# One decoder layer on one core: x and the first weights loaded in alternating pieces, the low-rank gate product behind the first chunk

## What is computed

```python
proj = h @ w_in
qa, ka, va, qg, kg, vg, rg, glr = jnp.split(proj, cuts, axis=-1)
log_a = jax.nn.log_sigmoid((glr @ w_gate_up + b_gate).astype(jnp.float32)) / GLA_GATE_TEMP
o = _gla(_heads(qg, GLA_HEADS), _heads(kg, GLA_HEADS), _heads(vg, GLA_HEADS), _heads(log_a, GLA_HEADS))
```

## Time and profile before

| | before |
|---|---|
| median of 3 runs | 429.07 us (428.97 to 429.78) |
| span of the profiled execution | 427.1 us |
| TensorE matmuls busy | 409.8 us, 96% |
| TensorE weight loads busy | 363.5 us, 85% |
| VectorE busy | 276.7 us, 65% |
| ScalarE busy | 195.3 us, 46% |
| POOL busy | 69.0 us, 16% |
| transferred | 75.64 MB, mean 177 GB/s |

### The profile page before, as it was taken

How to read it: one execution, slowest core, us unless ns; L and a number is a source line. 1 busy time by engine, 2 the same in 40 slices (tenths; PEclk the granted TensorE clock), 3 DMA queues, 4 the chain that set the end, 5 groups by cost and what they waited for, 6 DMA issues and landing times.

```text
span 427.1 us, 6338 instructions
## 1 busy us (share of the span) xinstructions
PE 409.8 (96%) x2576; PEld 363.5 (85%) x2576; DVE 276.7 (65%) x322; ACT 195.3 (46%) x243; POOL 69.0 (16%) x62
## 2 busy tenths in 40 slices
PE   7899999998999999799999999999999999999993
PEld 2899977888988888699988689898989898989882
DVE  2638377798596699966766875554555546372727
ACT  4644486843335637326543626344343444444400
POOL 1092000019681104100005220000000000000005
PEclk9899999999999999999999999999999999999997
DMA  8985638555146282274544264647373746555002
GB/s 244 397 326 190 206 101 293 185 198 167 44 142 261 93 282 110 92 264 140 196 152 144 100 196 165 231 146 248 106 265 122 231 162 200 193 172 221 0 2 98
DMA packets 33159, 75.64 MB, mean 177 GB/s; under 512 B 2528, under 2 KB 5104, under 8 KB 33136
## 3 DMA queue, kind: packets, MB, share of 16 engines
q1 hardware_dynamic: 31776, 75.18, 50.8%
q10 hardware_dynamic: 1360, 0.15, 0.3%
HBM read 74.27 MB, written 1.05 MB: 176 GB/s over the span
## 4 chain that ended last, share of the span: by engine, by line
PE 64%; DVE 5%; ACT 3%; issue 2%; POOL 1%; DVEq 0%; ACTq 0%
PE bank L1204 20%; PE bank L1206 20%; PE bank L1205 20%; DVE w_lo L797 1%; ACT w_hi L509 1%; PE bank L1360 1%; ACT again L656 1%; POOL actA_lo L483 1%; DVE X L1010 1%; DVE X L1016 1%; DVE actA_lo L1035 1%; ACT actA_hi L661 1%; DVE stats L998 0%; PE bank L1418 0%; DVE X L993 0%
## 5 line engine op out<-in xcount | busy, mean ns | idle before, releaser
L797 DVE TENSOR_TENSOR w_lo<-raw,w_hi 128x2048 fp32r<-128x2048 f32 x36 | 83.8, 2334 | 31.0 <-ACT w_hi L509 31.0
L1204 PE MATMUL bank<-actA_hi,w_hi 128*128 128x256 f32 x352 | 99.9, 284 | 0.6 <-DVE actA_lo L1035 0.6
L1205 PE MATMUL bank<-actA_lo,w_hi 128*128 128x256 f32 x352 | 99.6, 283 | 0.0
L1206 PE MATMUL bank<-actA_hi,w_lo 128*128 128x256 f32 x352 | 99.6, 283 | 0.0
L1138 DVE TENSOR_TENSOR w_lo<-raw,w_hi 128x2048 fp32r<-128x2048 f32 x24 | 55.0, 2291 | 44.8 <-ACT w_hi L739 44.8
L509 ACT CAST w_hi<-raw 128x2048 fp32r<-128x2048 f32 x38 | 72.1, 1912 | 16.5 <-PE bank L1206 14.2
L1204 PE MATMUL bank<-w_hi,actB_hi 128*128 128x512 f32 x192 | 75.5, 393 | 0.0
L1205 PE MATMUL bank<-w_lo,actB_hi 128*128 128x512 f32 x192 | 74.8, 390 | 0.0
L1206 PE MATMUL bank<-w_hi,actB_lo 128*128 128x512 f32 x192 | 74.7, 389 | 0.0
L1204 PEld LDWEIGHTS bank<-actA_hi,w_hi 128*128 128x128 f32 x352 | 67.5, 192 | 1.6 <-issue 1.3
L1205 PEld LDWEIGHTS bank<-actA_lo,w_hi 128*128 128x128 f32 x352 | 67.5, 192 | 0.3
(11 more groups left out here) (174 smaller groups left out, 599.6 us busy)
## 6 DMA issues: line engine op xcount, KB each, us to landing
raw<-in_w_ff SPq DMA_DIRECT2D x32, 1024.0 KB, 5.2
raw<-in_w_in SPq DMA_DIRECT2D x10, 1024.0 KB, 8.1
raw<-in_w_xkv SPq DMA_DIRECT2D x8, 1024.0 KB, 5.1
raw<-in_w_mix_o SPq DMA_DIRECT2D x4, 1024.0 KB, 4.9
raw<-in_w_xq SPq DMA_DIRECT2D x4, 1024.0 KB, 5.4
raw<-in_w_xo SPq DMA_DIRECT2D x4, 1024.0 KB, 5.0
raw<-in_w_in SPq DMA_DIRECT2D x4, 512.0 KB, 9.3
probs<-in_ln_g SPq DMA_DIRECT2D x3, 512.0 KB, 6.2
```

The costliest lines, as they stand in the source:

```text
L797: dve.tensor_tensor(dst, half_view(u), hi_part.bitcast(f32), ALU.subtract).then_inc(lo_done, 1)
L1204: pe.matmul(dst, stat[0], mov[0], start=start, stop=False)
L1205: pe.matmul(dst, stat[0], mov[1], start=False, stop=False)
L1206: return pe.matmul(dst, stat[1], mov[0], start=False, stop=stop)
```

## The change

It does five things.

- SP loads x in four pieces of 0.25 MB and chunk 0 in four pieces of 0.5 MB, alternating. The list `EARLY_CUTS` says in which pieces ScalarE and VectorE split them, and `early_count` which count of the counters belongs to a piece. TensorE works through chunk 0 k by k, all four column groups of one k together; high x high and high x low of a k are ahead of the wait for that k's low weights.
- The low-rank product goes behind chunk 0. Its weights come from the host as a contiguous array `w_glr`, and are split in high and low: 16 columns each in a stationary tile of 128 columns whose rest POOL has set to zero. TensorE makes 16 matmuls in f32r with the split x. The result has 32 rows, high and low, and `w_gate_up` is loaded twice, one below the other, so that `z` adds both.
- `z` goes from ahead of `qa0` to behind it. ScalarE's and VectorE's lists follow: ScalarE casts unit 5 ahead of the evacuation of `qa0` and of Exp, and unit 6 behind Ln; VectorE subtracts unit 5 ahead of the bias adds, and unit 6 behind the scan.
- SP's load of unit 4 no longer waits for the low-rank product, but for the subtraction of the last piece of x.
- WARM_UP is 3.

```diff
-WARM_UP = 2
+WARM_UP = 3
...
+EARLY_CUTS = []
+for _p in range(4):
+    EARLY_CUTS.append((0, 2 * _p, 512 * _p, 512 * _p + 512))
+    for _a in range(2 if _p == 0 else 1):
+        _n = 512 if _p == 0 else 1024
+        EARLY_CUTS.append((1 + _p // 2, 2 * _p + 1, 1024 * (_p % 2) + _n * _a, 1024 * (_p % 2) + _n * _a + _n))
...
+def early_count(u, column):
+
+    return 1 + [(cut[0], cut[3]) for cut in EARLY_CUTS].index((u, column))
...
-        def wait_lo(eng, u, piece=1):
+        def wait_lo(eng, u):
 
             if u < EARLY:
-                eng.wait_ge(early_lo, 2 * u + piece + 1)
+                eng.wait_ge(early_lo, early_count(u, 2048))
...
                 if u >= RAW:
                     wait_lo(sp, u - RAW)
-                if u == RAW:
-                    sp.wait_ge(bank_full[FILL["glr"][0]], 1)
...
-            for u in range(EARLY):
-                src = xT.rearrange("(a p) s -> p a s", p=P) if u == 0 else chunk_source(0, u - 1)
-                tiles = src.shape[1] // 2
-                for piece in range(2):
-                    sp.dma_start(raw[:, u, piece * 1024:(piece + 1) * 1024].rearrange("p (a n) -> p a n", a=tiles),
-                                 src[:, piece * tiles:(piece + 1) * tiles, :]).then_inc(early_in[2 * u + piece], 16)
+            for p in range(4):
+                sp.dma_start(raw[:, 0, 512 * p:512 * p + 512].rearrange("p (a s) -> p a s", a=2),
+                             xT.rearrange("(a p) s -> p a s", p=P)[:, 2 * p:2 * p + 2, :]).then_inc(early_in[2 * p], 16)
+                sp.dma_start(raw[:, 1 + p // 2, 1024 * (p % 2):1024 * (p % 2) + 1024].rearrange("p (a n) -> p a n", a=2),
+                             chunk_source(0, p // 2)[:, 2 * (p % 2):2 * (p % 2) + 2, :]).then_inc(early_in[2 * p + 1], 16)
...
+            pool.memset(wglr_split.bitcast(f32), 0.0).then_inc(wglr_zeroed, 1)
...
-            act.dma_start(wglr[:], w_in[:, GL:GL + RANK].rearrange("(a p) n -> p a n", p=P)).then_inc(wglr_in, 16)
+            act.dma_start(wglr[:].rearrange("p a n -> p (a n)"), w_glr).then_inc(wglr_in, 16)
             act.wait_ge(half_done, 1)
             act.copy(diag[:], minus_half[:])
-            act.dma_start(wgu[:], w_gate_up).then_inc(wgu_in, 16)
+            for n in range(2):
+                act.dma_start(wgu[n * RANK:(n + 1) * RANK, :], w_gate_up).then_inc(wgu_in, 16)
...
+            for u, dma, a, b in EARLY_CUTS:
+                act.wait_ge(early_in[dma], 16)
+                act.copy(first_hi[u][:, a:b], raw[:, u, a:b]).then_inc(early_hi, 1)
+            act.wait_ge(wglr_in, 16)
+            act.wait_ge(wglr_zeroed, 1)
+            act.copy(wglr_split[:, :, 0:RANK], wglr[:]).then_inc(wglr_hi, 1)
             hi_half(1, 0)
-            wait_full(act, "glr")
-            act.copy(glrT[:], bank[4][0:RANK, 0:S]).then_inc(freed("glr"), 1)
             hi_half(1, 1)
             evacuate("qg", qgT, DK ** -0.5)
             evacuate("kg", kgT)
+            wait_full(act, "glr")
+            act.copy(glrT[:], bank[4][0:2 * RANK, 0:S]).then_inc(freed("glr"), 1)
+            hi_half(2, 0)
+            evacuate("qa0", qaT[:, 0:2, :].rearrange("p m s -> p (m s)"))
             act.wait_ge(zabs_done, 1)
             act.activation(zabs, zabs, ACT.Exp, scale=-1.0).then_inc(act_link, 1)
             act.wait_ge(act_link, 1)
             act.activation(zabs, zabs, ACT.Ln, bias=1.0).then_inc(softplus_done, 1)
-            for n in range(2):
-                hi_half(2, n)
-                evacuate(f"qa{n}", qaT[:, 2 * n:2 * n + 2, :].rearrange("p m s -> p (m s)"))
+            hi_half(2, 1)
+            evacuate("qa1", qaT[:, 2:4, :].rearrange("p m s -> p (m s)"))
...
+            for n, (u, _, a, b) in enumerate(EARLY_CUTS):
+                dve.wait_ge(early_hi, n + 1)
+                dve.tensor_tensor(first_lo[u][:, a:b], raw[:, u, a:b], first_hi[u][:, a:b].bitcast(f32), ALU.subtract)\
+                    .then_inc(early_lo, 1)
+            dve.wait_ge(wglr_hi, 1)
+            dve.tensor_tensor(wglr_split[:, :, RANK:2 * RANK], wglr[:], wglr_split[:, :, 0:RANK].bitcast(f32),
+                              ALU.subtract).then_inc(wglr_lo, 1)
             lo_half(1, 0)
             lo_half(1, 1)
+            lo_half(2, 0)
...
             dve.scalar_tensor_tensor(zabs, zlin, -1.0, zlin, ALU.mult, ALU.max).then_inc(zabs_done, 1)
-            lo_half(2, 0)
-            lo_half(2, 1)
...
             dve.tensor_tensor_scan(cum, reset[:], zlin, 0.0, ALU.mult, ALU.add).then_inc(cum_done, 1)
+            lo_half(2, 1)
...
+            banks = [begin("qg"), begin("kg")]
+            for k in range(8):
+                unit_w, end = 1 + k // 4, 512 * (k % 4) + 512
+                if k >= 2:
+                    end = 1024 * (k % 4 // 2) + 1024
+                if k < 2 or k % 2 == 0:
+                    pe.wait_ge(early_lo, early_count(0, 512 * (k // 2) + 512))
+                    pe.wait_ge(early_hi, early_count(unit_w, end))
+                stat = [weight(0, k, m * P, (m + 1) * P) for m in range(4)]
+                dst = [banks[m // 2][:, (m % 2) * S:(m % 2 + 1) * S] for m in range(4)]
+                for m in range(4):
+                    pe.matmul(dst[m], stat[m][0], actA_hi[:, k, :], start=k == 0 and m % 2 == 0, stop=False,
+                              skip_group_check=True)
+                    pe.matmul(dst[m], stat[m][0], actA_lo[:, k, :], start=False, stop=False, skip_group_check=True)
+                if k < 2 or k % 2 == 0:
+                    pe.wait_ge(early_lo, early_count(unit_w, end))
+                for m in range(4):
+                    i = pe.matmul(dst[m], stat[m][1], actA_hi[:, k, :], start=False, stop=k == 7, skip_group_check=True)
...
             b = begin("glr")
-            pe.wait_ge(wglr_in, 16)
+            pe.wait_ge(wglr_lo, 1)
             for k in range(8):
...
+                pe.matmul(b[:, 0:S], wglr_split[:, k, :], actA_hi[:, k, :], start=k == 0, stop=False)
+                i = pe.matmul(b[:, 0:S], wglr_split[:, k, :], actA_lo[:, k, :], start=False, stop=k == 7)
             i.then_inc(full("glr"), 1)
...
+            features(1, 0, A, "qa0")
             b = begin("z")
             wait_out(pe, "glr")
-            pe.wait_ge(wgu_in, 16)
+            pe.wait_ge(wgu_in, 32)
...
-            features(1, 0, A, "qa0")
             features(1, 1, A, "qa1")
```

More of the change, by code:

```diff
@@ L154, in build @@
         wglr = sb("wglr", [P, 8, RANK])
-        wgu = sb("wgu", [RANK, 256])
-        glrT = sb("glrT", [RANK, S])
+        wgu = sb("wgu", [2 * RANK, 256])
+        glrT = sb("glrT", [2 * RANK, S])
         bgate = sb("bgate", [P, 2])
@@ L240, in build @@
         lev_q = [v[:, :].rearrange("p (a r s) -> p a r s", a=4, r=2) for v in (reset, qkdiag)]
+        wglr_split = shared("probs", 0, 1024).rearrange("p (k n) -> p k n", k=8)
         def level_mask(n):
@@ L252, in build @@
         lo_done = sem("lo_done")
-        early_in = [sem(f"early_in{n}") for n in range(2 * EARLY)]
+        early_in = [sem(f"early_in{n}") for n in range(8)]
+        wglr_zeroed, wglr_hi, wglr_lo = map(sem, ("wglr_zeroed", "wglr_hi", "wglr_lo"))
         early_hi, early_lo = sem("early_hi"), sem("early_lo")
@@ L802, in _ @@
             flat = "p a s -> p (a s)"
-            for u, (whole, hi_part) in enumerate(zip(early(actA_lo, w_lo), early(actA_hi, w_hi))):
-                for piece in range(2):
-                    cut = slice(piece * 1024, (piece + 1) * 1024)
-                    dve.wait_ge(early_hi, 2 * u + piece + 1)
-                    dve.tensor_tensor(whole[:, cut], raw[:, u, cut], hi_part[:, cut].bitcast(f32), ALU.subtract)\
-                        .then_inc(early_lo, 1)
+            first_hi, first_lo = early(actA_hi, w_hi), early(actA_lo, w_lo)
+            for n, (u, _, a, b) in enumerate(EARLY_CUTS):
[5 more added lines that the diff above has]
+                              ALU.subtract).then_inc(wglr_lo, 1)
             lo_half(1, 0)
             lo_half(1, 1)
+            lo_half(2, 0)
             dve.wait_ge(small_in, 32)
@@ L1263, in _ @@
                 pe.matmul(bank[7][:, :], reset[:, 0:P], reset[:, :], start=True, stop=True)
+            banks = [begin("qg"), begin("kg")]
[16 more added lines that the diff above has]
+                    i = pe.matmul(dst[m], stat[m][1], actA_hi[:, k, :], start=False, stop=k == 7, skip_group_check=True)
+                    if k == 7 and m % 2 == 1:
+                        i.then_inc(full(("qg", "kg")[m // 2]), 1)
@@ L1266, in _ @@
             b = begin("glr")
-            pe.wait_ge(wglr_in, 16)
+            pe.wait_ge(wglr_lo, 1)
             for k in range(8):
-                if k % 4 == 0:
-                    pe.wait_ge(early_in[k // 4], 16)
-                i = pe.matmul(b[0:RANK, 0:S], wglr[:, k, :], raw[:, 0, k * S:(k + 1) * S], start=k == 0, stop=k == 7)
+                pe.matmul(b[:, 0:S], wglr_split[:, k, :], actA_hi[:, k, :], start=k == 0, stop=False)
```

(18 more changed lines are left out.)

9 lines of the change are left out of this document (3 added, 6 removed).

## The result

The changed kernel takes 431.89 us in the median of eight runs (431.03 to 433.58), the kernel before 429.24 (428.97 to 430.33). The ratio is 1.0059, with a 95% interval of 1.0037 to 1.008: slower by some 2.6 us, where 0.3 us less was forecast. Of all executions behind this document two, one each of the experiments "before, gate late" and "changed, only gnorm late", took 2297 and 1038 us; the cause is not known, and they are left out of every median and ratio. The profiled execution has a span of 430.5 us (432.25 us with what lies around it), against 427.1.

What follows compares the result with a forecast made beforehand. TensorE, busy 409.8 of 427.1 us, was taken as the bound. After waits of 1.75 and 1.73 us, 0.30 us of gain was left: 429.07 - 0.30, rounded to 428.8 us; 8-in-10 range 427.4 to 430.5.

Steps and rivals of the forecast that it cites:

- The start: Start of chunk 0: with three warm-up products the warm-up decides, and the first matmul comes at 7.1 us.
- For the pieces I go by bytes.: First loads: landings interpolated by bytes from the old order; second pair in at 9.55, TensorE waiting 0.7 us for it.
- Clock full from then to 40 us.: Sign of being right: TensorE's granted clock full from the first f32r matmul at 7.1 to 40 us.
- First wait, unit 4: Twelve matmuls into `qa0`: unit 4, issued at 15.0, lands at 20.0; TensorE stands 1.75 us and resumes at 24.65.
- Second wait, the gate's chain: Ahead of k = 4 of `ka0`: 9.99 us from `z` through unit 6's subtraction, so TensorE stands 1.73 us.
- the row that I went by: Unit 4's subtraction beside POOL's bias work: 0.30 us longer, not a wait for a whole 1.34 us instruction.
- The sum to k = 4 of ka0: That matmul begins at 38.96 us, against 39.26 before: 0.30 us gained.
- From there both kernels do the same work.: Behind k = 4 of `ka0`: same work, same order, loads waiting on the same subtractions; differences arising after 45 us excluded.
- It decides somewhere between 1.8 and 2.7: Gap length in us that lets the clock fall: it fell behind 2.7 and not behind 1.8 at `transpose_x`.
- (3): Rival: the clock falls behind the first new wait, inside `qa0`, costing 1.5 us; 430.3 us, chance 0.16.
- (1): Rival: unit 4 lands at 19.3 and misses POOL, 1.0 us more gain; 427.8 us, chance 0.24.
- (2): Rival: the gate's chain is no bound, the second wait is hidden, 2.0 us gained; 427.0 us, chance 0.08.

Runs made afterwards that it cites:

- before, gate late: The kernel before with only the change's gate order: `z` behind `qa0`, unit 5 subtracted ahead of the bias adds, unit 6 behind Ln and scan; 431.29 us, ratio 1.0048.
- changed, only gnorm late: The changed kernel with the `gnorm` load alone issued behind the first casts, `wgu` and `bgate` staying ahead; 431.18 us, ratio 1.0027.
- Small loads late: The changed kernel with ScalarE's four small loads (both `wgu` copies, `bgate`, `gnorm`) issued behind the casts of the first pieces; 430.81 us, ratio 1.0025.
- unit 6 early: The changed kernel with the cast and subtraction of unit 6 moved back ahead of the gate's Exp, Ln and scan; 429.35 us, ratio 0.9996.
- the gap filled: The changed kernel with two idle products between k = 1 and k = 2 of chunk 0, in the 2.36 us gap; 432.05 us, ratio 1.0084.
- the kernel before with the small loads late: The kernel before with its `wgu`, `bgate` and `gnorm` loads issued behind the casts of the first six pieces; 425.90 us, ratio 0.9919.
- the whole reordering mended: The changed kernel with small loads behind the first casts, unit 4 loaded in halves, and unit 6 ahead of Exp, Ln and scan; 424.59 us, ratio 0.9885.

## Why the prediction was wrong

By its own steps:

- **The start.** Forecast 7.1, measured 6.48: right, and the warm-up did end early. (The 9 us that "look available at the start" are no term of the sum, and too many: its own walk gains 25.1 - 21.4 = 3.7.)
- **"For the pieces I go by bytes."** This step failed. The second pair was to be in at 9.55 and was cast at 10.76, so TensorE stood for 2.36 us where 0.7 was forecast. The sum took the landings of the old order as a rate and spread the bytes evenly over it; it did not look at what else was under way in that stretch. Small loads late shows the cause: without them the piece is cast at 7.61. Three of the four small issues stood in the trace of before; the prediction takes only the added `wgu` issue into account, as hidden behind the first loads. They held up the kernel before too, by 1.6 us at its third piece (9.55, and 7.95 without them), and the changed kernel by 3.15.
- **"Clock full from then to 40 us."** Failed as a consequence. A gap of 2.36 us is near the 2.66 behind which the clock had fallen, and it fell. It need not have: behind the 2.04 us at the same place in the profile with unit 6 early it didn't. Chunk 0 ended at 22.3, not 19.5: 1.2 from the piece, 1.6 from the clock.
- **First wait, unit 4.** Issue forecast at 15.0, and the row of the two issues ends at 16.13, so about 15.8; landing 5.0 us later, as taken; cast at 20.74 for 20.0; subtraction 2.52 for 2.59, ready at 25.2 for 24.6. The mechanism was right, and later by the late piece. Its wait didn't show only because TensorE was later still, and it shows in the profiles in which the clock stayed up in chunk 0 (1.27 us with unit 6 early, 2.25 us with the gap filled).
- **z.** 30.00 for 28.97: 1.0 us, the balance of these. Unit 4's low part, ready at 25.2, would by itself have put `z` at 25.25 + 36 x 0.12 = 29.6; the other 0.4 is TensorE's own lateness.
- **Second wait, the gate's chain.** Forecast 9.99 us, measured 30.00 to 40.83 = 10.83, and it cost what was said and more: 2.33 for 1.73 us. The term mis-sized is `zlin`, 1.78 us for 0.68. It began at 35.56, 0.07 behind POOL's `qkdiag` (35.49). In the kernel before, `qkdiag` was over 4 us ahead of `zlin` (37.60):

```profile
32.04 1.29 POOL L424 TENSOR_TENSOR qkdiag<-gla 128x512 f32<-128x512 f32 x1
```

  The order that the change makes brings these two near each other, but whether they meet is a matter of tenths: with the gate's order alone and in the changed kernel filled `zlin` began 0.2 us behind the end of `qkdiag` and took 0.69. SBUF — State Buffer (Who interferes with whom) in the Trainium skill says that a VectorE operation with two SBUF inputs contends with a GpSimd operation that reads SBUF, and that the port pair they share is an exclusive lock. This row, 1.10 us longer beside an instruction of 1.29, comes near a wait for the whole of it, while the row that I went by showed 0.30. I let one row speak against the rule, where it was only a milder case.
- **The sum to k = 4 of ka0.** -0.30, +1.03 from `z`, +0.84 from the chain: 1.57, and 1.57 was measured. Of the 2.95 us by which the medians missed the forecast (+2.65 for -0.30) that is 1.87; the other 1.1 arose behind this place, and I put it down to the falls below.
- **"From there both kernels do the same work."** True, but not in the same time. The profile of the changed kernel has one fall of the clock more, 1.6 us at 108.6. The forecast treated the clock as a matter of the changed stage and the median as a fixed number; the runs show that it differs from one execution to the next. "It decides somewhere between 1.8 and 2.7" read one draw as a threshold: four profiles have a fall behind that same gap of 1.8 us, at 173 to 178.
- **Rivals.** (3), the fall behind the first new wait, is not what happened here, but it is what the changed kernel filled does. (1) and (2) did not come. The chance of slower, 0.20, was too small: two waits stood in the sum as certain, a gain of 0.3 us was all that was left above them, and a late landing or a contention adds to them in full. The range ended at 430.5 with the dearest single mishap; two together were not in it.

What stays open: how small loads of 97 KB together more than halve the rate of the large ones for a microsecond or two (where their packets queue was not tried), why they cost the alternating order twice what they cost the order before, and the half microsecond by which the changed kernel, at an equal number of falls, is slower than the 1.57 us of the profile.

## What to carry to other kernels

Ahead of a reordering of first loads, look at the small loads that share their stretch: here three lines moved behind the first casts gave 3.4 us, the whole reordering mended 1.3 more, and the reordering as it was lost 2.6. When work is moved to start sooner, follow the two loads behind it and every chain that is moved past a step TensorE needs, since both took the gain back here. A gap of 1.5 us or more in TensorE's work cost its length here, and in some executions up to 1.6 us more; where it can't be closed, idle products in it are worth trying (1.2 us in the kernel before), but not where a later wait takes the gain, as unit 4's did in the changed kernel.

## What the runs showed of the hardware

The granted clock of TensorE fell to 0.50 for stretches of 3.4 us behind gaps of 1.54 to 2.66 us, in some profiles and not in others; the times of 31 runs of one kernel form four groups, 427.2 to 427.7, 428.8 to 429.4, 430.3 to 430.5 and 431.2 to 431.4 us, and their mean clocks go with them. It fell behind a gap of 1.54 us (at 108.6 in the changed kernel), and not behind one of 2.45 (the gate's order alone, where chunk 0 ran at full clock). At a gap of 3.24 us it fell while TensorE still stood, and was down for 6.8 us.

A VectorE operation with two SBUF inputs took up to 1.1 us longer beside POOL's `qkdiag`: 1.78 for 0.68 in `zlin`, in the changed kernel and again in the kernel before with the small loads late. Where it began 0.2 us behind the end of `qkdiag` it took 0.69.

Four small loads of 97 KB together, issued between 1.3 and 3.1 us among the large ones, brought the rate between 7 and 8 us from 378 down to 152 GB/s, and the piece that was then under way was cast 3 us later.
